# Turning the rows of the next rest within the current rest, in a mixture-of-experts tail on one core

## What is computed

```python
def run_block(args):
    e, toks, wts = args
    xb = h2[toks]
    hid = jax.nn.silu(xb @ w_gate[e]) * (xb @ w_up[e])
    return (hid @ w_down[e]) * wts[:, None]
```

## Time and profile before

| | |
|---|---|
| median of 3 runs | 1282.3 us (1277.6 to 1284.46) |
| the profiled execution | 1274.56 us |
| its span, first to last instruction | 1272.8 us |
| TensorE busy | 1168.1 us (92%) |
| mean granted TensorE clock | 0.968 |
| `down(15)` ends, last fixed matmul | 1171.0 us into the span |
| `yo` of rest 4 starts | 1254.65 us |

### The profile page before, as it was taken

How to read it: one execution, slowest core, us unless ns; L and a number is a source line. 1 busy time by engine, 2 the same in 40 slices (tenths; PEclk the granted TensorE clock), 3 DMA queues, 4 the chain that set the end, 5 groups by cost and what they waited for, 6 DMA issues and landing times. The chain is left out here.

```text
span 1272.8 us, 24039 instructions
## 1 busy us (share of the span) xinstructions
PE 1168.1 (92%) x9806; PEld 657.6 (52%) x9806; DVE 549.4 (43%) x1308; ACT 307.1 (24%) x789; POOL 201.5 (16%) x248
## 2 busy tenths in 40 slices
PE   6999999999997899999999997399999999998883
PEld 5534444444444676899954555144444444443441
DVE  4368355999793565556733446011311111111010
ACT  5153116322213677334421222000000000000000
POOL 0201310300001333000000012301012423321121
PEclk9999999999998899999999998699999999999987
DMA  9311531322203723345408315589999999989861
GB/s 318 102 35 48 179 74 48 115 84 100 50 33 105 171 86 107 90 146 148 140 18 293 140 67 199 199 308 367 363 344 371 334 372 347 374 330 314 346 213 67
DMA packets 110886, 240.03 MB, mean 189 GB/s; under 512 B 36532, under 2 KB 71812, under 8 KB 105400
## 3 DMA queue, kind: packets, MB, share of 16 engines
q1 hardware_dynamic: 84136, 150.30, 33.4%
q0 software_dynamic: 16608, 48.33, 10.7%
q10 hardware_dynamic: 10032, 39.85, 9.5%
HBM read 208.89 MB, written 36.10 MB: 192 GB/s over the span
## 5 line engine op out<-in xcount | busy, mean ns | idle before, releaser
L503 PE MATMUL pj_ps<-hT,pj_w 128*128 128x512 f32 x576 | 252.9, 595 | 0.0
L503 PEld LDWEIGHTS pj_ps<-hT,pj_w 128*128 128x128 f32 x576 | 107.8, 190 | 135.4 <-issue 134.9
L1397 PE MATMUL ps_out<-w_out,mixT 128*128 128x512 f32 x256 | 112.3, 594 | 2.1 <-PEq L2282 1.8
L2017 PE MATMUL ex_py<-wd,ex_hT 128*128 128x512 f32 x256 | 112.6, 592 | 1.0 <-DVE proj L2148 1.0
L2179 DVE TENSOR_TENSOR ex_hid<-ex_pu,ex_sg 128x512 f32<-128x512 f32 x16 | 11.1, 691 | 205.5 <-PE ex_pu L2037 205.5
L2105 ACT ACTIVATE ex_sg<-ex_pg 128x512 f32<-128x512 f32 x16 | 9.6, 597 | 317.9 <-PE ex_pg L2029 317.9
L2029 PE MATMUL ex_pg<-proj 128*128 128x512 f32 x176 | 78.9, 602 | 1.3 <-DVE proj L2141 1.3
L713 DVE RECIPROCAL mixT<-mixT 128x1024 f32<-128x1024 f32 (+1 forms) x11 | 68.9, 6262 | 22.5 <-ACT mixT L633 17.5
L1397 PEld LDWEIGHTS ps_out<-w_out,mixT 128*128 128x128 f32 x256 | 47.8, 190 | 59.5 <-issue 59.4
L2037 PE MATMUL ex_pu<-proj 128*128 128x512 f32 x176 | 77.3, 592 | 0.0
L2017 PEld LDWEIGHTS ex_py<-wd,ex_hT 128*128 128x128 f32 x256 | 47.5, 190 | 55.3 <-issue 54.0
(11 more groups left out here) (319 smaller groups left out, 1933.4 us busy)
## 6 DMA issues: line engine op xcount, KB each, us to landing
wd<-in_moe_w_down ACTq DMA_DIRECT2D x19, 2048.0 KB, 9.9
proj<-in_moe_w_gate SPq DMA_DIRECT2D x14, 2048.0 KB, 10.4
proj<-in_moe_w_up SPq DMA_DIRECT2D x14, 2048.0 KB, 9.2
mixT<-in_moe_w_gate SPq DMA_DIRECT2D x7, 2048.0 KB, 10.2
mixT<-in_moe_w_up SPq DMA_DIRECT2D x7, 2048.0 KB, 9.1
pj_w<-in_w_in SPq DMA_DIRECT2D x18, 512.0 KB, 3.7
products<-pj_unit POOLq DMA_DIRECT2D x4, 2048.0 KB, 9.8
proj<-products SPq DMA_DIRECT2D x32, 256.0 KB, 3.7
```

Of the source, the lines that this page charges most:

```text
L503: mm = pe.matmul(ps[:, t % 2, half, :], w_tile(t)[:, n, :], s.hT[:, n, half * 512:(half + 1) * 512], start=(n == 0), stop=(n == KD - 1))
L1397: mm = pe.matmul(s.ps_out[:, t % 2, half * 512:(half + 1) * 512], s.mixT[:, k, t * P:(t + 1) * P], s.w_out[:, k, half * 512:(half + 1) * 5 ...
L2017: mm = pe.matmul(py[:, half, :], hT[:, j, :], wd[e % 2][:, j, half * 512:(half + 1) * 512], start=(j == 0), stop=(j == KF - 1))
```

## The change

It touches TensorE's and VectorE's queues only.

- Rest b no longer begins with its own 8 transposes. It turns the rows of rest b+1: four transposes after its up matmuls, ahead of the 2 transposes of `ph`, and four behind those, ahead of the down matmuls. VectorE copies `pt` to `xoT` between `hido` and `yo` of rest b.
- The rows of rest 0 are turned before the loop, between `turn_h(15)` and `down(15)`, and copied ahead of `finish(15)`.
- TensorE loads the number of rests ahead of `down(15)`, and the five waits behind it are gone.

```diff
+        def overflow_count(eng):
             eng.wait_ge(tables, 1)
-            n = eng.value_load(s.blk[0:1, 2 * NOV:2 * NOV + 1], min_val=0, max_val=NOV)
+            return eng.value_load(s.blk[0:1, 2 * NOV:2 * NOV + 1], min_val=0, max_val=NOV)
...
+            def turn_rows(u, part):
+                for j in range(4 * part, 4 * part + 4):
+                    mm = pe.transpose(pt[:, j // 4, (j % 4) * P:(j % 4 + 1) * P], xo[:, u, j * P:(j + 1) * P], s.ident)
+                return mm
+
             turn_h(NE - 1)
+            pe.wait_ge(xo_in[0], 16)
+            turn_rows(0, 0)
+            turn_rows(0, 1).then_inc(xo_turned, 1)
+            n = overflow_count(pe)
             down(NE - 1)
-            pe.wait_ge(x_copied, NE)
-            pe.wait_ge(hidden, NE)
-            pe.wait_ge(silu, NE)
-            pe.wait_ge(h_copied, NE)
-            pe.wait_ge(summed, NE)
...
-                pe.wait_ge(xo_in[u], i * 16 + 16)
-                pe.wait_ge(xo_copied, b + 1)
-                for j in range(KD):
-                    mm = pe.transpose(pt[:, j // 4, (j % 4) * P:(j % 4 + 1) * P], xo[:, u, j * P:(j + 1) * P], s.ident)
-                mm.then_inc(xo_turned, 1)
                 pe.wait_ge(xo_copied, b + 2)
...
                 mm.then_inc(upped, 1)
+                pe.wait_ge(xo_in[1 - u], (i + u) * 16 + 16)
+                turn_rows(1 - u, 0)
                 pe.wait_ge(hidden_o, b + 2)
...
                 mm.then_inc(ho_turned, 1)
+                turn_rows(1 - u, 1).then_inc(xo_turned, 1)
...
-            finish(NE - 1)
...
             dve.sem_inc(hidden_o, 1)
+            dve.wait_ge(xo_turned, 2)
+            copy_rows()
+            finish(NE - 1)
...
-                dve.wait_ge(xo_turned, b + 2)
-                dve.wait_ge(upped, b + NE)
-                dve.tensor_copy(xoT[:, :, :].rearrange("p (a j) r -> p a j r", a=2), pt[:, :, :].rearrange("p a (j r) -> p a j r", j=4)[:, :, :, 0:ROW]).then_inc(xo_copied, 1)
...
                 dve.tensor_tensor(hido[:, :], pu[:, 0:256], sgo[:, :], ALU.mult).then_inc(hidden_o, 1)
+                dve.wait_ge(xo_turned, b + 3)
+                copy_rows()
                 dve.wait_ge(downed, b + (NE + 1))
```

More of the change, by code:

```diff
@@ L1883, in experts, with overflow @@
         block = c.enter_context(nc.Block())
-        def overflow(eng, body):
+        def overflow_count(eng):
             eng.wait_ge(tables, 1)
-            n = eng.value_load(s.blk[0:1, 2 * NOV:2 * NOV + 1], min_val=0, max_val=NOV)
+            return eng.value_load(s.blk[0:1, 2 * NOV:2 * NOV + 1], min_val=0, max_val=NOV)
+        def overflow(eng, body, n=None):
+            n = overflow_count(eng) if n is None else n
             with eng.Fori(0, TURNS) as i:
@@ L2087, in block_of_rows @@
                 mm.then_inc(downed, 1)
-            overflow(pe, block_of_rows)
+            overflow(pe, block_of_rows, n)
         @block.scalar
@@ L2187, in _, with copy_rows @@
                     overflow_rows()
-            finish(NE - 1)
+            def copy_rows():
+                dve.tensor_copy(xoT[:, :, :].rearrange("p (a j) r -> p a j r", a=2), pt[:, :, :].rearrange("p a (j r) -> p a j r", j=4)[:, :, :, 0:ROW]).then_inc(xo_copied, 1)
             dve.sem_inc(xo_copied, 1)
             dve.sem_inc(hidden_o, 1)
+            dve.wait_ge(xo_turned, 2)
+            copy_rows()
+            finish(NE - 1)
             dve.sem_inc(summed_o, 1)
```

## The result

The changed kernel takes **1270.86 us** (median of 6 executions, 1267.46 to 1273.59), the kernel before 1278.49 on the same chip: a ratio of **0.9941**, 95% interval 0.9919 to 0.9963. That is a saving of 7.6 us (4.7 to 10.4), where 13.4 were forecast. The time lies in the range, the direction is right, and somewhat over half of the saving came (57%; 35 to 78% by the interval).

A forecast was written before the change was run, and what follows sets the result against it. TensorE's chain of waits bounds; after the fixed experts, GpSimd's loop bounds beside loads, then TensorE's. `yo` of rest 4 moves from 1254.65 to 1241.25, 13.4 us; 1282.3 - 13.4 = 1268.9 us, range 1262.5 to 1277.

The forecast's parts named there:

- The entry: From `down(15)` to gate of rest 0: gate starts 5.1 us earlier, with `down(15)` starting 0.4 us later.
- The clock in rest 0: First gate no longer runs at the lower clock after idling: 3.67 us instead of 6.06, saving 2.4 us.
- The read of rest 0: GpSimd's read, now beside weight loads, lands in 6.5 us (3.4 to 9.3); `yo` of rest 0 at 1185.3.
- the first rival: TensorE's loop bounds all rests, reads land at their median: 21.8 us saved, 1260.5 us; chance 0.10.
- TensorE's loop of 12.2 us: TensorE's time per rest with the next rows' transposes filling gaps: 12.2 us (12.1 to 12.4), against 14.0.
- Link 1: GpSimd's way from `yo` of rest 0 to `yo` of rest 1, beside weight loads: 18.4 us, as before.
- The clock's fall: In rest 2, after TensorE idles 5.1 us, the lower clock level again, costing 2 us.
- Rest 2: TensorE idles 5.1 us behind up; down weights land at 1210.5, and down ends at 1216.5.
- the signs for wrong: `down(15)` over 1 us late, second link over 15 us, rest 1 or 2 idle far over 5, late clock fall.
- The second one: Rival: contention stays for a second link of GpSimd's loop; 5.4 us saved, 1276.9 us; chance 0.16.
- The fourth: Rival: rest 0's gathered rows are late for the turn ahead of `down(15)`; entry gives back 2.7, 1271.6 us; chance 0.05.
- GpSimd's loop: From `yo` through write and next read to next `yo`: 18.4 us beside weight loads, 10.9 without; next to bound.

The follow-up runs named there:

- e2_entry_only: Change's part ahead of `down(15)` only; in a rest, next rows turned behind down and copied behind `yo`; 0.9954 to the kernel before.
- e11_down_first: Change, with rest 3's gate and up loads held until rest 1's down weights land, rest 4's until rest 1's read lands; 0.9985 to the kernel before.
- e13_entry_first: Entry alone, with rest 3's gate/up loads held for rest 1's down weights, rest 4's for rest 1's read; 1.0039 to the kernel before.

## Why the prediction came out as it did

Times behind the start of `turn_h(15)`, forecast and measured, for `yo` of rests 0 to 4: 23.0, 41.4, 54.3, 66.5, 79.0 against 26.1, 49.4, 61.7, 73.6, 86.6. The stretch lacks 7.6 us of the forecast (13.4 less 5.8; that the measured saving of the medians is 7.6 too is chance). They stand in the first two numbers: 3.1 and then 4.9; the three links behind them took 37.2, forecast 37.6.

- **The entry: right.** Gate of rest 0 starts 8.67 us behind `turn_h(15)`, 14.3 before: 5.6 saved, forecast 5.1. The 0.4 us on `down(15)` didn't come: it starts 1.63 us behind `turn_h(15)` in both kernels, and its wait is for VectorE's `finish(14)` in both. The register load ran from 1165.3 to 1166.1, while the matmuls of `down(14)` still ran, so it isn't in the way.
- **The clock in rest 0: right**, 2.4 us (6.06 to 3.67).
- **The read of rest 0: mis-sized, inside its bounds.** It landed after 9.1 us, where I took 6.5 out of 3.4 to 9.3, and went out 0.9 later than before, 0.5 later than forecast, since the write of expert 15 took 4.3 and not 3.4. By the time that it ran, ScalarE's load (1184.78) was beside it as well, and from 1188 to 1191 us three queues had nearly equal numbers of packets, those of GpSimd and ScalarE of 4 KB:

```profile
q1 hardware_dynamic: 52, 0.85, 66.5%
q0 software_dynamic: 51, 0.21, 17.0%
q10 hardware_dynamic: 47, 0.19, 15.6%
```

2.6 and 0.5 are the 3.1. The argument for a place nearer to the middle counted the queues and not the length of their packets. (Of the reads before, four of five took 3.4 and not three, as the first rival has it.)

- **TensorE's loop of 12.2 us: right** where nothing is late: gates at 1216.28 and 1228.44. The transposes cost nothing there that shows, and the ones of rest 1 waited 0.70 us for their gather.
- **Link 1 and rest 1: the step that failed.** I priced TensorE's rest 1 at 12.2 us with "up to 1.3 later" for a gather, and never asked when its down weights would land. I did ask that for rest 2, with 16.5 us from the earlier trace rows, and put TensorE's idle time there. The link took 23.3 us instead of 18.4. GpSimd's side of it was as forecast: the read of rest 1 landed at 1204.90 + 6.5 = 1211.4, 18.2 us behind `yo` of rest 0, and with rest 4's loads held back the whole link took 19.1. TensorE's side, priced as the shorter, bounded. In the kernel before, the transposes and the wait for the copy held back SyncE's next loads too, and I moved these loads forward in the sum only as traffic beside the read, not as traffic beside the down weights. The four loads come within 16 us now (17.6 before), with a shorter gap between the pairs, and the fifth load, with its short runs, has to outlast them.
- **The clock's fall** came, for the reason given (a long idle stretch) and at the price given (5.74 for 3.65), one rest early:

```profile
1205.00:1210.00 5.00, 0.00 (x0) 0.00 (x0) 0.00 (x0) 0.00 (x0) 2.19 (x4) 0.50 0.98 407
1210.00:1215.00 5.00, 4.28 (x11) 1.39 (x13) 0.00 (x0) 0.00 (x0) 0.00 (x0) 0.50 1.03 349
```

(us, busy PE, PEld, DVE, ACT, POOL, then granted clock, DMA share, GB/s: TensorE idle at a full DMA.)

- **Rest 2: right by luck.** The link to `yo` of rest 2 was forecast at 12.9 us and took 12.3, but for another reason. The forecast had TensorE idle for 5.1 us behind up, and down at the lower clock. Neither came: rest 1 was so late that gather and weights of rest 2 were there, and TensorE's loop ran through at full clock.
- **The signs and the total.** Of the signs for wrong, one came: an idle stretch in rest 1 far longer than 5 us. That the time is only 2.0 us from the forecast of 1268.9 is luck in part: 5.8 us of the saving are missing, but the kernel before took 1278.49 this time, 3.8 less than the 1282.3 that the forecast started from.
- **The rivals.** The second one, contention staying longer, was nearest (5.4 saved, 5.8 measured in the stretch); its mechanism was not the one at work, since what stayed late was a weight load and not GpSimd's transfers. The fourth didn't come: the gather of rest 0 landed at 1151.29 + 14.0 = 1165.3, 2.2 us ahead of its use. Behind the starved load, GpSimd's loop was indeed next: with rest 4 held back the stretch is 81.2, 2.2 from the forecast 79.0.

The change's two parts, then: the entry carries all of what was saved. The turning within the rests is worth nothing as the loads stand, and together with rest 4's loads held back it gives 5.4 us (86.6 to 81.2, one profile each; 0.9954 to 0.9919, with overlapping intervals). The entry alone with the same hold wasn't run; that the hold by itself gives little there, since no down load is starved in `e2_entry_only`, is argued and not shown. Under the two waits of `e11_down_first` and `e13_entry_first` the turning is worth 0.5%.

What stays open: whether a version exists in which neither the down weights nor GpSimd's transfers are late. None of the orders tried had it.

## What to carry to other kernels

When an edit takes a wait or a step out, list what it had been holding back: here it paced the next loads, and they took the engines from a transfer that had just been in time. Before counting a TensorE loop at its own length, write down for each of its operands, in each turn, issue time plus landing time beside the new traffic. And where two queues load at once, compare the lengths of their runs: the one with short ones gets the smaller share.

## What was not expected of the hardware

A load of 2 MB took 8.0 to 11.8 us to land with nothing in SyncE's queue and 25.9 to 31.8 beside four of SyncE's loads. Queues shared by packets: 222 to 211 and 212 to 213 packets in 10 us, at 15.2 and 4.0 KB each. Lengthening one queue's runs moved time to the next queue: at 4, 8 and 16 KB the down load of rest 1 took 25.9, 20.9 and 17.3 us and the gather of rest 2 9.7, 13.7 and 17.5, and the ratio of the whole didn't move by more than its interval. And TensorE's load of a register from SBUF (0.49 us and its arithmetic), written between transposes and matmuls, ran ahead of both, under earlier matmuls, and cost no time that the trace shows.
